# Attention logits issued in pairs, the scores and forget gate of a recurrent block reordered with early output products, and one weight split three steps later

## The reference

```python
# first block
proj = rmsnorm(x) @ w_in
o_a = hgrn2(q, f, i, g)        # 4 heads, gated linear attention, head size 64
o_b = rglru(xb, gb)            # width 512: convolution, two gates, a linear recurrence
o_c = gla(q, k, v, g, g_lr)    # 4 heads, key size 32; log_f = log_sigmoid(g_lr @ w_g_up + b_g) / 16
x = x + concat(o_a, o_b, o_c) @ w_out
x = x + (gelu(conv(h @ w_gate)) * (h @ w_val)) @ w_down
x = rmsnorm(x)
# second block, two layers
x = layer_norm(alpha * x + 0.5 * swiglu(x))
x = layer_norm(alpha * x + concat(window(a), mla(b), axial(c), diff(d)) @ w_out)
x = layer_norm(alpha * x + 0.5 * swiglu(x))
```

## Time and profile before

| what | value |
|---|---|
| median of 3 runs | 1468.13 us (1465.68 to 1469.3) |
| profiled execution, its time | 1464.74 us |
| its span, first to last instruction | 1463.1 us |
| TensorE busy | 1379.1 us, 94% |
| VectorE, ScalarE, GpSimd busy | 920.1, 726.1, 92.6 us |
| mean granted TensorE clock | 0.963 |
| 16 DMA engines | 51.2% of the span in the main queue |

### The profile page before, as it was taken

How to read it: one execution, slowest core, us unless ns; L and a number is a source line. 1 busy time by engine, 2 the same in 40 slices (tenths; PEclk the granted TensorE clock), 3 DMA queues, 4 the chain that set the end, 5 groups by cost and what they waited for, 6 DMA issues and landing times.

```text
span 1463.1 us, 20466 instructions
## 1 busy us (share of the span) xinstructions
PE 1379.1 (94%) x8222; PEld 1211.8 (83%) x8222; DVE 920.1 (63%) x1343; ACT 726.1 (50%) x1141; POOL 92.6 (6%) x137
## 2 busy tenths in 40 slices
PE   6899799998899999998899999899999999899997
PEld 6788788887788888987888888788888888888886
DVE  3787666776765666636665656756568446666656
ACT  5556355555455553545255555455553545355452
POOL 1233000000000000500000000000001400000000
PEclk9798899999999998999899999999999999899999
DMA  7223366666476563330566566475654331375561
GB/s 226 87 90 128 87 203 200 188 199 196 118 230 199 173 189 106 116 116 30 149 187 202 188 199 186 153 209 173 200 164 145 104 116 50 114 235 179 181 201 50
DMA packets 301191, 229.17 MB, mean 157 GB/s; under 512 B 13083, under 2 KB 283818, under 8 KB 301098
## 3 DMA queue, kind: packets, MB, share of 16 engines
q1 hardware_dynamic: 301082, 227.88, 51.2%
q10 hardware_dynamic: 16, 0.00, 0.0%
HBM read 226.80 MB, written 1.05 MB: 156 GB/s over the span
## 4 chain that ended last, share of the span: by engine, by line
PE 74%; DVE 14%; ACT 7%; DMA 3%; issue 1%; POOL 0%; SPq 0%; ACTq 0%; DVEq 0%
PE bank L855 20%; PE bank L783 11%; PE bank L784 11%; PE bank L785 11%; PE bank L858 10%; DVE lo_gu L1630 5%; ACT hi_gu L1292 4%; PE bank L1198 2%; PE bank L1168 2%; PE bank L985 2%; DVE lo_dn L1635 1%; DMA st_dn<-in_ffn_w_down 1%; DVE conv L1782 1%; PE bank L1178 1%; DVE stats L1657 1%
## 5 line engine op out<-in xcount | busy, mean ns | idle before, releaser
L855 PE MATMUL bank<-xT,hi_gu 128*128 128x512 f32 x1616 | 405.8, 393 | 4.8 <-DVE lo_gu L1630 4.0
L1630 DVE TENSOR_TENSOR lo_gu<-st_gu,hi_gu 128x2048 fp32r<-128x2048 f32 (+2 forms) x146 | 323.9, 2221 | 122.6 <-ACT hi_gu L1292 122.6
L855 PEld LDWEIGHTS bank<-xT,hi_gu 128*128 128x128 f32 x1616 | 297.5, 189 | 64.4 <-DVE lo_gu L1630 6.2
L1292 ACT ACTIVATE hi_gu<-st_gu 128x2048 fp32r<-128x2048 f32 (+3 forms) x147 | 270.4, 1843 | 18.5 <-PE bank L785 10.1
L858 PEld LDWEIGHTS bank<-xT,lo_gu 128*128 128x128 f32 x1616 | 221.5, 191 | 16.0
L858 PE MATMUL bank<-xT,lo_gu 128*128 128x256 f32 x1616 | 226.1, 283 | 0.0
L783 PE MATMUL bank<-hi_dn,actTh 128*128 128x512 f32 x436 | 172.0, 394 | 6.7 <-DVE actTl L1764 4.4
L784 PE MATMUL bank<-lo_dn,actTh 128*128 128x512 f32 x436 | 170.9, 392 | 0.0
L785 PE MATMUL bank<-hi_dn,actTl 128*128 128x512 f32 x436 | 169.7, 389 | 0.0
L1785 DVE TENSOR_TENSOR act<-act,bank 128x256 f32<-128x256 f32 x101 | 42.5, 421 | 173.2 <-ACT act L1378 173.2
L1299 ACT ACTIVATE hi_dn<-st_dn 128x1024 fp32r<-128x1024 f32 x109 | 114.6, 1056 | 67.2 <-DMA st_dn<-in_ffn_w_down 67.2
(11 more groups left out here) (269 smaller groups left out, 1844.2 us busy)
## 6 DMA issues: line engine op xcount, KB each, us to landing
st_gu<-in_ffn_w_gu SPq DMA_DIRECT2D x176, 512.0 KB, 5.1
st_dn<-in_ffn_w_down SPq DMA_DIRECT2D x109, 512.0 KB, 6.6
st_gu<-in_w_in SPq DMA_DIRECT2D x23, 1024.0 KB, 5.3
st_gu<-in_w_out SPq DMA_DIRECT2D x12, 1024.0 KB, 5.1
st_gu<-in_ffn_w_gate SPq DMA_DIRECT2D x21, 512.0 KB, 3.9
st_gu<-in_ffn_w_val SPq DMA_DIRECT2D x21, 512.0 KB, 5.3
st_gu<-in_w_in SPq DMA_DIRECT2D x10, 512.0 KB, 4.4
gb<-in_ln_g SPq DMA_DIRECT2D x6, 512.0 KB, 7.2
```

The source lines that it names most:

```text
L855: pe.matmul(b[:, :], hv[:, w, k, :], xT[:, k, :, :].rearrange("p a b -> p (a b)"), start=k == 0, stop=k == KD - 1, skip_group_check=True)
L1292: i = act.activation(high, staged, ACT.Copy)
L1630: i = dve.tensor_tensor(low, staged, high.bitcast(F32), ALU.subtract)
```

## The change

- `UNITS` runs over token tiles outside and head pairs inside, so units u and u + 1 (u even) are two head pairs of one token tile, in different partitions.
- `logits(u)` makes the logits of u and u + 1 together, alternating between their banks, and waits for the exponentials of both u - 3 and u - 2. It is called in even steps only, and once ahead of the loop.
- `scores` issues the four 64-row heads first, then the four 32-row heads.
- The first scores wait for the scaled gates (`forget_in`) instead of the cumulated sums.
- ScalarE copies the low-rank rows, after its high split of chunk 4. VectorE scales the forget gates ahead of the low split of chunk 4, and does that of chunk 5 after line 1841 and its scaling. The first half of chunk 0 of the loop no longer waits for `z_in`; the second half does.
- The first block's output product is split: blocks 2 to 5 of its first two chunks (48 of 192 matmuls) are made straight after the head products; their other blocks and the other two chunks follow behind the heads' transposes.
- `("out2", l, 3)` is split after step 12 on ScalarE and 13 on VectorE.

```diff
-UNITS = [(kind, m, pr) for kind in KINDS for pr in range(4 if kind == "dif" else 2) for m in range(M)]
+UNITS = [(kind, m, pr) for kind in KINDS for m in range(M) for pr in range(4 if kind == "dif" else 2)]
...
-            pe.wait_ge(t_copied_v.sem, t_copied_v["lr"])
+            pe.wait_ge(t_copied_a.sem, t_copied_a["lr"])
...
                         if j == 0:
-                            pe.wait_ge(t_copied_v.sem, t_copied_v["lr"])
-                            pe.wait_ge(z_in.sem, z_in[0])
+                            if z == 1:
+                                pe.wait_ge(z_in.sem, z_in[0])
...
-                for r in range(3):
-                    for b in range(4):
-                        if r < len(BANK_HEADS[b]):
...
+                for b, r in ((0, 0), (1, 0), (0, 1), (1, 1), (0, 2), (2, 0), (1, 2), (3, 0)):
+                    head, base, rws, blk = BANK_HEADS[b][r]
...
-            pe.wait_ge(cum_ok.sem, cum_ok[0])
+            pe.wait_ge(forget_in.sem, forget_in[0])
...
+            pe.wait_ge(mix_low.sem, mix_low["lru"])
+            early = ((0, 0), (1, 0), (0, 1), (1, 1))
+            for m, j in early:
+                out_part(m, j, (2, 3, 4, 5))
             for j in range(4):
                 if j == 0:
                     pe.wait_ge(heads_ok.sem, heads_ok[1])
...
-            out_product("out", 0)
+            for m, j in early:
+                out_part(m, j, (0, 1, 6, 7))
+            for m, j in ((0, 2), (0, 3), (1, 2), (1, 3)):
+                token_half(CHUNK_NO["out", 0, j], m, bank[2 * m + 1][:, (j % 2) * WCOLS:(j % 2 + 1) * WCOLS])
...
-                    if u < LOGIT_BANKS:
...
+                    for v in (u, u + 1):
+                        if v < LOGIT_BANKS:
...
+                        else:
+                            pe.wait_ge(exp_ok.sem, exp_ok[l, v - LOGIT_BANKS])
...
                     for z in range(2):
...
+                        for v in (u, u + 1):
+                            pr = UNITS[v][2]
...
+                            t = pe.matmul(bank[v % LOGIT_BANKS][:, z * S:(z + 1) * S], q_, k_, start=not biased, stop=True, skip_group_check=biased)
+                            if z == 1:
+                                t.then_inc(logits_ok.sem, logits_ok.one((l, v)))
...
                 logits(0)
                 half(4, 0)
-                logits(1)
                 half(4, 1)
...
-                    if s + 2 < units:
+                    if s + 2 < units and s % 2 == 0:
                         logits(s + 2)
...
+            act.wait_ge(t_done.sem, t_done[3, 0])
+            act.activation(lr[0:LR_RANK, :], bank[6][0:LR_RANK, 0:S], ACT.Copy).then_inc(t_copied_a.sem, t_copied_a.one("lr"))
             weights_high(5)
...
-            dve.wait_ge(t_done.sem, t_done[3, 0])
-            dve.tensor_copy(lr[0:LR_RANK, :], bank[6][0:LR_RANK, 0:S]).then_inc(t_copied_v.sem, t_copied_v.one("lr"))
-            weights_low(4)
-            weights_low(5)
...
             dve.tensor_scalar(lf[:, 0:2, :], lf[:, 0:2, :], F_FLOOR, None, ALU.max).then_inc(forget_in.sem, forget_in.one(0))
+            weights_low(4)
             dve.wait_ge(z_done.sem, z_done[0])
...
             dve.tensor_scalar(z3, z2, 0.0, 1.0 / 16, ALU.min, ALU.mult).then_inc(own_v.sem, own_v.one())
+            weights_low(5)
...
```

More of the change, by code:

```diff
@@ L979, in scores @@
                 qq, kk = (gq, gk) if lev == 0 else (qs[:, lev % 2], ks[:, lev % 2])
-                for r in range(3):
-                    for b in range(4):
-                        if r < len(BANK_HEADS[b]):
[L983 to L986, removed]
+                for b, r in ((0, 0), (1, 0), (0, 1), (1, 1), (0, 2), (2, 0), (1, 2), (3, 0)):
+                    head, base, rws, blk = BANK_HEADS[b][r]
+                    bk, c0 = slot_of(b, r, pr)
+                    i = pe.matmul(bank[bk][:, c0:c0 + P], kk[base:base + rws, blk, kt * P:(kt + 1) * P],
+                                  qq[base:base + rws, blk, qt * P:(qt + 1) * P], start=True, stop=True)
                 i.then_inc(scored.sem, scored.one((lev, pr)))
@@ L1152, in logits @@
                         pe.wait_ge(qk_copied.sem, qk_copied[l, "mla", 1, 2])
+                    kind, m, _ = UNITS[u]
+                    ts = slice(m * P, (m + 1) * P)
                     biased = kind in ("win", "dif")
                     if biased:
-                        for z in range(2):
-                            pe.matmul(b[:, z * S:(z + 1) * S], slopes[:, 2 * pr + z if kind == "win" else 4 + pr, :],
-                                      distances[:, m, 0 if kind == "win" else 1, :], start=(z == 0), stop=False, skip_group_check=True)
@@ L1159, in logits @@
-                    for z in range(2):
-                        if kind == "mla":
-                            q_, k_ = mlaq[0:96, 2 * pr + z, ts], mlak[0:96, 2 * pr + z, :]
-                        elif kind == "dif":
-                            rows_ = slice(32 * pr, 32 * pr + 32)
-                            q_, k_ = difq[rows_, z, ts], difk[rows_, z, :]
-                        else:
-                            rows_ = slice(64 * pr, 64 * pr + 64)
-                            q_, k_ = (winq, axq)[kind == "ax"][rows_, z, ts], (wink, axk)[kind == "ax"][rows_, :]
-                        t = pe.matmul(b[:, z * S:(z + 1) * S], q_, k_, start=not biased, stop=True, skip_group_check=biased)
@@ L1169, in logits @@
-                    t.then_inc(logits_ok.sem, logits_ok.one((l, u)))
+                        for v in (u, u + 1):
+                            pr = UNITS[v][2]
+                            for z in range(2):
+                                pe.matmul(bank[v % LOGIT_BANKS][:, z * S:(z + 1) * S], slopes[:, 2 * pr + z if kind == "win" else 4 + pr, :],
+                                          distances[:, m, 0 if kind == "win" else 1, :], start=(z == 0), stop=False, skip_group_check=True)
+                    for z in range(2):
+                        for v in (u, u + 1):
+                            pr = UNITS[v][2]
+                            if kind == "mla":
+                                q_, k_ = mlaq[0:96, 2 * pr + z, ts], mlak[0:96, 2 * pr + z, :]
+                            elif kind == "dif":
+                                rows_ = slice(32 * pr, 32 * pr + 32)
+                                q_, k_ = difq[rows_, z, ts], difk[rows_, z, :]
+                            else:
+                                rows_ = slice(64 * pr, 64 * pr + 64)
+                                q_, k_ = (winq, axq)[kind == "ax"][rows_, z, ts], (wink, axk)[kind == "ax"][rows_, :]
+                            t = pe.matmul(bank[v % LOGIT_BANKS][:, z * S:(z + 1) * S], q_, k_, start=not biased, stop=True, skip_group_check=biased)
+                            if z == 1:
+                                t.then_inc(logits_ok.sem, logits_ok.one((l, v)))
```

28 lines of the change are left out of this document (15 added, 13 removed).

## The result

The changed kernel took 1446.29 us in the median of 4 runs (1441.63 to 1448.83), the kernel before 1466.91 beside it. The ratio is 0.9861 with an interval of 0.9833 to 0.9888: faster, by 20.6 us (1.4%) where 32.8 were forecast, and inside the range. The profiled execution took 1441.63 us, with a span of 1440.0 and a mean clock of 0.971. It is the fastest of the four; the others had mean clocks of 0.965 to 0.967.

What follows compares the result with a forecast made beforehand. TensorE, busy 94% of the span, was taken as the bound. First block -11.6 and attention -21.2 us made -32.8: 1431.9 us on the profile's scale, 1435.3 on the median's, with a range of 1423 to 1454.

Steps and rivals of the forecast that it cites:

- rival (a): Attention: paired logits don't overlap, only visits to narrow shapes halve; total -19 us, 1449; chance 13%.
- rival (b): First block gives little: ScalarE and VectorE set its pace, early products at half clock; total -26.5 us, 1441.6; chance 14%.
- Part 1: First block's start, forget gate and first scores: chunk 0 starts near 40, scans end at 48.75 instead of 53.35; -4.6 us.
- Part 2: First block's scores: grouping heads of one shape saves 0.42 us a call, only partly on the path; -2.0 us.
- the reading by serial weight loads: Scores: 32 weight loads one after another at 0.107 us each would take 3.4 us, so reordering wins nothing.
- Part 3: First block's end: 48 early output matmuls fill TensorE's wait for the heads, product ends at 172.9 against 178.8; -5.0 us.
- Part 4: Attention: 8 logit pairs a layer save 9.3 us, empty odd steps and step 14 cost 3.6 and 1.4; net -4.3 a layer.
- Part 5: Attention: moving the w_out split three steps removes a 3.69 us TensorE stall and 2.6 of lost clock; -6.3 us a layer.
- rival (c): Attention: idle odd steps from 9 on let the clock fall, 20 us of work a layer at half clock; 1475 us; 4%.

Runs made afterwards that it cites:

- norm first: Changed kernel with VectorE beginning the first block's second norm before the low splits of the feed-forward's first two chunks; 1437.32 us, ratio 0.9832.
- split only: Kernel before the change with only the fourth attention output chunk's split moved to after steps 12 and 13; 1456.83 us, ratio 0.9924.
- attention only: Kernel before the change with the whole attention part (unit order, paired logits, moved split) on the old first block; 1455.99 us, ratio 0.9922.
- no early products: Changed kernel with the first block's output product whole again behind the heads' transposes; 1442.50 us, ratio 0.9830.

## Why the prediction was right, and where it was off

**Sign and range.** Right: every part that was to make TensorE's work shorter did, and the likeliest value was 11 us too low. That the time still fell inside the range is in part luck: the slow side of the range was there for rivals (a) and (b), and what filled it was something else. The measured gain of 20.6 lies next to rival (a)'s 19, but the pairs do overlap; the first block gave 6.1 where rival (b) had 5.3, but not because of ScalarE's pace or half clock.

**Part 1 (-4.6).** Right. Chunk 0 starts at 40.20 (forecast near 40), the scans end at 48.46 (48.75), 4.9 us earlier.

**Part 2 (-2.0).** The price of a call was mis-sized in one direction, its place on the path in the other. A call is 1.08 us (two take 2.15, from 102.36 to the next product at 104.51), not 1.27. In stretches of 0.04 us of the changed kernel's scores (length, TensorE busy, clock, DMA share, GB/s), the eight records of four 32-row heads stand together:

```profile
103.22:103.26 0.04, 0.04 (x8) 1.00 0.00 0
103.26:103.30 0.04, 0.04 (x8) 1.00 0.00 0
```

Thus the reading by serial weight loads falls. The Trainium skill ("TensorEngine Tiling (Array Packing)", Key Properties) says that a change of tiling mode drains the engine. By it I had 1.06 a call, and the runs show 1.08. But the old order costs only 1.0 us at the feed-forward, not 2, and nothing at the last scores: levels 4 to 8 must follow VectorE and ScalarE for the most part.

**Part 3 (-5.0).** The step that failed was not in the part but behind it. The product itself gained more than forecast: from the last scores, 5.1 us ahead, to its end, 11.3 ahead, makes 6.2, the bound I had given for both waits gone; my own working, 178.8 to 172.9, had said 5.9. The clock was back at 1.00 by 144, after some 3 us of the early products as forecast, and stayed there; the heads were ready when their turn came, and only 1.27 us of waiting was left (stretches of the changed kernel):

```profile
145.70:146.00 0.30, 0.30 (x5) 0.30 (x4) 0.30 (x1) 0.00 (x0) 0.00 (x0) 1.00 0.00 0
...
149.93:167.50 17.57, 17.54 (x144) 17.33 (x144) 10.54 (x8) 8.04 (x5) 0.00 (x0) 1.00 0.63 181
```

But "172.9, against 178.8" was carried to the end of the kernel without asking who needed the product next. It was the norm, third in VectorE's queue behind a split that waits for a load. In the kernel before it stood there too, hidden. Of 11.3 us 5.2 were lost there; "norm first" brought 4.7 back.

**Part 4 (-4.3 a layer).** In layer 1, without half clock in the changed kernel (0.01 us lost, 4.33 before), 11.9 us split into: clock -4.3 (2.6 behind the stall, which part 5 had, and 1.7 for the fall 50 to 55 us into the layer, which no part had); the stall -3.6; new waits +4.2 (0.45, 0.87, 0.25, 1.21, 0.69 and 0.69); and the rest, the pairs, -8.2. Layer 0 gives -8.1 for the pairs. Forecast were -9.3 and +5.0, so the net is as forecast; 1.21 in step 14 stood for my 1.4, and 0.87 in step 9 for 0.87.

**Part 5 (-6.3 a layer).** "3.69 and 2.6 of clock" was right for the split alone: both go in both layers of "split only", less the new 0.93. What failed is the sum with part 4: the new wait of step 14 was priced at 1.4 us of waiting, and the clock behind it at nothing. On top of the pairs it exchanged 4.8 us of wait for 1.21, and a fall of the clock behind it that costs 4.7 in layer 0 of the changed kernel and more in "attention only". There half clock took 3.3 and 3.8 us more than in the kernel before, where I had counted 2.6 less: 12 us over two layers, which makes -21.2 into -9, and the two layers of "attention only" were 8.8 us shorter. The changed kernel's profile shows -20.9 because its layer 1 was spared. I had priced step 14 at the wait alone, and had seen a fall in the odd steps only as rival (c), with 20 us of work a layer at half clock or nothing, no matter where. In fact it comes in some layers and lasts 10 to 20 us. What the Trainium skill ("TensorE: Matmul & The Clock Gate", Part 4) says of transposes, which I had set beside (c), was put to no test: no run here parts them from the short products among which they stand.

**The sum.** Attention was forecast within 0.3 us of the profile and some 12 too high for an execution with both falls; the first block was forecast 5.5 too high, 4.7 to 5.1 of it for the norm's place. The other 4 us by which the profiles fall short (23.1 us where 32.8 were forecast) are the 4.6 of the untouched feed-forwards, less the 0.9 of the last one.

## What to carry to other kernels

When work moves earlier, follow it to its consumer and read what stands ahead of that consumer in its engine's queue; a wait that was hidden is the next bound. Pair small products only where they lie in different rows of the array, and leave the full ones single as cover for the steps between. Rate a new wait amid short products not by its length alone but by what the granted clock does behind it, over several executions: the mean clock of each timed run shows without a profile that it was lower, though not where.

## What was not expected of the hardware

- Two gains that were each some 11 to 14 us alone were together 11.4 (ratio 0.9922, interval 0.9895 to 0.9949). Only both together make a wait of 1.2 us in step 14, and behind it (1.3 with the earlier split) the clock was at 0.50 for 10 to 20 us in 11 of 18 layers, in some and not in others of the same kernel.
- Groups of the same shape follow each other without the loss that a change of shape brings: two calls of the scores went from 3.44 to 2.23 us by order alone, 0.6 a call, with the four 32-row heads side by side.
- The clock fell without any wait too: at 625 in the kernel before, for 3.4 us, with TensorE busy for all of the time from 616 to 632. With the logits in pairs it did not fall there.
- The clock came back during the first of the early products, by 144, where they follow the head products without a wait. Without them ("no early products") the stretch from 146 to 150 was still at 0.50, as in the kernel before.
